# Low parts in four pieces, the second u sooner, a joint first block and sample attention four batches at a time, in a split-fp32 decoder layer

## The reference, cut to what is computed

```
h = h + 0.5 * post1(SwiGLU_1(pre1(h)))
u = pre_m(h);  [qA kA vA qB kB vB gA gB] = u @ w_in
h = h + post_m((sigmoid(gA) * (oA @ p_a) + sigmoid(gB) * (oB @ p_b)) @ w_o)
h = h + 0.5 * post2(SwiGLU_2(pre2(h)))

# oA: dilated sliding-window attention, 3 groups of 4 heads
# oB: stick-breaking attention, 8 heads
# for each of the 8 sample tokens (one per batch): the same two, over
#   211 cached rows of A in three groups, and 2 pages of 128 rows of B
#   found in a page table
```

## Time and profile before

| | |
|---|---|
| median of 3 runs | 1332.63 us (1331.58 to 1333.54) |
| profiled execution | 1329.96 us |
| its span | 1328.1 us |
| mean granted PE clock in it | 0.986 |

### The profile page before, as it was taken

How to read it: one execution, slowest core, us unless ns; L and a number is a source line. 1 busy time by engine, 2 the same in 40 slices (tenths; PEclk the granted TensorE clock), 3 DMA queues, 4 the chain that set the end, 5 groups by cost and what they waited for, 6 DMA issues and landing times.

```text
span 1328.1 us, 24643 instructions
## 1 busy us (share of the span) xinstructions
PE 1271.6 (96%) x10504; PEld 1230.2 (93%) x10504; DVE 555.8 (42%) x925; ACT 411.4 (31%) x683; POOL 453.3 (34%) x131
## 2 busy tenths in 40 slices
PE   6989999999998999999999999998989999999996
PEld 6979999999998999999988888998979999999995
DVE  3373242421226550455377400859484242321225
ACT  6232222122224242345455412244332212222221
POOL 2223334444443233221413312251233444444441
PEclk8989999999998999999999999999999999999998
DMA  5112222222222223312222454221112222222311
GB/s 194 64 64 96 95 95 95 95 79 96 88 76 108 78 85 115 98 33 96 82 79 77 133 189 159 95 96 64 64 64 96 95 95 87 76 84 97 108 57 65
DMA packets 30674, 123.25 MB, mean 93 GB/s; under 512 B 4506, under 2 KB 12722, under 8 KB 18994
## 3 DMA queue, kind: packets, MB, share of 16 engines
q1 hardware_dynamic: 30594, 122.09, 26.5%
HBM read 115.39 MB, written 6.67 MB: 92 GB/s over the span
## 4 chain that ended last, share of the span: by engine, by line
PE 84%; DVE 8%; DVEq 3%; ACT 1%; DMA 1%; issue 1%; POOL 1%; SPq 0%; POOLq 0%; ACTq 0%
PE bank L1398 25%; PE bank L1399 24%; PE bank L1400 24%; DVEq L1043 3%; PE bank L1420 2%; PE bank L1577 1%; DVE u_lo L1059 1%; DVE tmp L1143 1%; PE bank L1766 1%; DVE hid_hi L1131 1%; PE bank L1619 1%; PE bank L1657 1%; PE bank L1606 1%; PE bank L1721 1%; PE bank L1634 1%
## 5 line engine op out<-in xcount | busy, mean ns | idle before, releaser
L580 POOL TENSOR_TENSOR w_lo<-raw,w_hi 128x2048 fp32r<-128x2048 f32 x89 | 409.9, 4607 | 800.3 <-ACT w_hi L647 602.7
L1398 PE MATMUL bank<-u_hi,w_hi 128*128 128x260 f32 x1952 | 562.9, 288 | 19.0 <-DVE u_lo L1059 15.1
L1399 PE MATMUL bank<-u_lo,w_hi 128*128 128x260 f32 x1952 | 553.1, 283 | 0.0
L1400 PE MATMUL bank<-u_hi,w_lo 128*128 128x260 f32 x1952 | 552.4, 283 | 0.0
L1398 PEld LDWEIGHTS bank<-u_hi,w_hi 128*128 128x128 f32 x1952 | 369.1, 189 | 32.5 <-issue 23.4
L1400 PEld LDWEIGHTS bank<-u_hi,w_lo 128*128 128x128 f32 x1952 | 369.7, 189 | 0.0
L1399 PEld LDWEIGHTS bank<-u_lo,w_hi 128*128 128x128 f32 x1952 | 369.4, 189 | 0.0
L647 ACT ACTIVATE w_hi<-raw 128x2048 fp32r<-128x2048 f32 x81 | 154.8, 1911 | 304.6 <-PE bank L1400 303.6
L1398 PE MATMUL bank<-hid_hi,w_hi 128*128 128x260 f32 x704 | 200.6, 285 | 0.5 <-POOL w_lo L594 0.5
L1399 PE MATMUL bank<-hid_lo,w_hi 128*128 128x260 f32 x704 | 200.0, 284 | 0.0
L1400 PE MATMUL bank<-hid_hi,w_lo 128*128 128x260 f32 x704 | 199.8, 284 | 0.0
(11 more groups left out here) (190 smaller groups left out, 1376.6 us busy)
## 6 DMA issues: line engine op xcount, KB each, us to landing
raw<-w_stream SPq DMA_DIRECT2D x84, 1024.0 KB, 4.8
raw<-w_stream SPq DMA_DIRECT2D x8, 768.0 KB, 4.2
e_raw<-w_stream SPq DMA_DIRECT2D x5, 1024.0 KB, 8.4
h<-x_t SPq DMA_DIRECT2D x8, 260.0 KB, 7.6
y_t<-h SPq DMA_DIRECT2D x8, 260.0 KB, 2.3
block<-kb_pool SPq DMA_DIRECT2D x8, 256.0 KB, 3.3
ring<-kb_pool SPq DMA_DIRECT2D x8, 256.0 KB, 3.0
ring<-vb_pool SPq DMA_DIRECT2D x8, 256.0 KB, 4.7
```

The lines of the kernel that those rows point to most:

```text
L580: pool.tensor_tensor(low, w_tiles(slot_of(n) if slot is None else slot)[0], top.bitcast(F32), ALU.subtract).then_inc(lo_made, 1)
L1398: pe.matmul(out, w, hi_x, start=first, stop=False)
L1399: pe.matmul(out, w, lo_x, start=False, stop=False)
L1400: return pe.matmul(out, v, hi_x, start=False, stop=last)
```

## The change

**First block.** x is loaded in four pieces for both groups, ACT and DVE make the high and the low part of u for 520 columns at once, and the first chunk is multiplied for all four banks in one pass over k. Its low parts and those of the second chunk are made by quarters on DVE (`first_lo_part`; ACT makes the high parts by the same quarters in `first_hi_part`). POOL begins with the third chunk.

**Pieces.** Each other low part is made on POOL by instructions of 128 x 512: four for a chunk, two for a half.

**Order on DVE.** In `ffn_up`, `up_scale` is split in the scaling (`up_scale`) and the product with sg (`up_gate`). u_again of group 0 stands after the first tile's hidden instead of the second's, and u_again of group 1 ahead of the last three up_gates. At QKV, u_again of group 1 stands behind all of project_scale(3, ...). `take_out` adds to acc before it writes f, and f's write, not acc's, is what releases the bank, as before.

**Sample attention.** The four batches of a round are the innermost loop in each of the four functions, so consecutive matmuls write at partitions 0, 32, 64 and 96; a call waits for all four batches' pages. Keys of A: one call for four batches at j = 2, 3; keys of B: one call for four batches and one page each at j = 4 to 7; values of A at j = 9, 10; values of B at j = 12 and after the loop. SP waits for a whole round before it loads ring again.

```diff
-            def load_x(g, s):
-                part = (slice(None), slice(2 * s, 2 * s + 2), tg(g))
-                sp.dma_start(h[part], x_t[part]).then_inc(x_in[4 * g + s], 16)
-
             sp.dma_start(gain[:], gains_in).then_inc(gain_in, 16)
             for s in range(4):
-                load_x(0, s)
+                part = (slice(None), slice(2 * s, 2 * s + 2), slice(None))
+                sp.dma_start(h[part], x_t[part]).then_inc(x_in[s], 16)
                 part = (slice(None), slice(s * CH // 4, (s + 1) * CH // 4))
                 sp.dma_start(e_raw[0][part], w_stream[0][part]).then_inc(first_in[s], 16)
             load_early(FFN1 + 1)
-            for s in range(4):
-                load_x(1, s)
             load(2, 0)
             load(3, 1)
...
                 if x >= 4:
-                    sp.wait_ge(ring_used, x - 3)
+                    sp.wait_ge(ring_used, 4)
                 sp.dma_start(ring[x % 4][:, 0:422], ka_cache[x]).then_inc(ring_in[x % 4], 16)
             def load_key_pages(y0, y1):
                 for y in range(y0, y1):
                     if y >= 8:
-                        sp.wait_ge(ring_used, y - 3)
-                        page(kb_pool, y, ring[y % 4], ring_in[y % 4])
+                        half, i = divmod(y - 8, 4)
+                        sp.wait_ge(ring_used, 8 + 4 * half)
+                        page(kb_pool, 8 + 2 * i + half, ring[i], ring_in[i])
                     else:
                         page(kb_pool, y, blocks[4 + y], page_in[y])
...
                     if y < 4:
-                        sp.wait_ge(ring_used, 13 + y)
+                        sp.wait_ge(ring_used, 16)
                     elif y == 4:
-                        sp.wait_ge(va_used, 1)
+                        sp.wait_ge(va_used, 4)
                     elif y >= 12:
-                        sp.wait_ge(ring_used, 17 + y - 12)
+                        sp.wait_ge(ring_used, 20)
                     page(vb_pool, y, blocks[y % 12], page_in[y - 4] if 4 <= y < 12 else ring_in[y % 4])
...
+            def low_part(slot, s, n):
+                src, top, low = w_tiles(slot)
+                a = slice(s * CH // n, (s + 1) * CH // n)
+                return pool.tensor_tensor(low[:, a], src[:, a], top[:, a].bitcast(F32), ALU.subtract)
+
             def lo(n, slot=None):
-                top, low = w_tiles(slot_of(n) if slot is None else slot)[1:]
+                slot = slot_of(n) if slot is None else slot
                 pool.wait_ge(hi_made, n + 1)
-                pool.tensor_tensor(low, w_tiles(slot_of(n) if slot is None else slot)[0], top.bitcast(F32),
-                                   ALU.subtract).then_inc(lo_made, 1)
+                for s in range(4):
+                    made = low_part(slot, s, 4)
+                made.then_inc(lo_made, 1)
...
                 pool.wait_ge(hi_half, count)
-                src, top, low = w_tiles(n % 2)
-                a, b = slice(0, CH // 2), slice(CH // 2, CH)
-                pool.tensor_tensor(low[:, a], src[:, a], top[:, a].bitcast(F32), ALU.subtract)
+                for s in range(2):
+                    low_part(n % 2, s, 4)
                 pool.wait_ge(hi_made, n + 1)
-                pool.tensor_tensor(low[:, b], src[:, b], top[:, b].bitcast(F32), ALU.subtract).then_inc(lo_made, 1)
+                for s in range(2, 4):
+                    made = low_part(n % 2, s, 4)
+                made.then_inc(lo_made, 1)
...
                 dve.wait_ge(post_sq, out_at(p, r, b) + 1)
-                dve.tensor_scalar(f[:, 2 * r + t, tg(g)], out_of(b), gain[:, 2 * p + 1, 2 * r + t:2 * r + t + 1],
-                                  None, ALU.mult).then_inc(read[b], 1)
                 if r == 0 and t == 0:
                     dve.tensor_copy(acc[:, g, :], sqa[:, b, :]).then_inc(acc_added, 1)
                 else:
                     dve.tensor_tensor(acc[:, g, :], acc[:, g, :], sqa[:, b, :], ALU.add).then_inc(acc_added, 1)
+                dve.tensor_scalar(f[:, 2 * r + t, tg(g)], out_of(b), gain[:, 2 * p + 1, 2 * r + t:2 * r + t + 1],
+                                  None, ALU.mult).then_inc(read[b], 1)
                 drain()
...
+            def up_scale(i, b, r):
                 dve.wait_ge(full[b], r + 2 * i + 2)
                 src = psum[b if i else first_bank(1, b)][:, 0:TG]
-                dve.tensor_tensor(x, src, rinv[:, g, :], ALU.mult).then_inc(read[b], 1)
+                dve.tensor_tensor(up_x[b], src, rinv[:, b // 2, :], ALU.mult).then_inc(read[b], 1)
+
+            def up_gate(q, i, b):
                 drain()
                 dve.wait_ge(sg_made, 8 * (q // 2) + 4 * i + b + 1)
-                dve.tensor_tensor(x, x, sg[:, b, :], ALU.mult)
-                hidden(i, b, x)
+                dve.tensor_tensor(up_x[b], up_x[b], sg[:, b, :], ALU.mult)
+                hidden(i, b, up_x[b])
...
-                    up_scale(q, 0, b, r0)
+                    up_scale(0, b, r0)
+                    up_gate(q, 0, b)
                 for b in range(4):
                     gate_scale(1, b, r0)
-                up_scale(q, 1, 0, r0)
-                up_scale(q, 1, 1, r0)
+                up_scale(1, 0, r0)
+                up_gate(q, 1, 0)
                 u_again(q, 0, r0 + FOLD)
-                up_scale(q, 1, 2, r0)
+                for b in range(1, 4):
+                    up_scale(1, b, r0)
                 u_again(q, 1, r0 + FOLD)
-                up_scale(q, 1, 3, r0)
+                for b in range(1, 4):
+                    up_gate(q, 1, b)
...
+            def first_lo_part(n, s):
+
+                dve.wait_ge(*((first_hi, 3 * n + s + 1) if s < 3 else (hi_made, n + 1)))
+                part = slice(s * CH // 4, (s + 1) * CH // 4)
+                src, top, low = w_tiles(slot_of(n))
+                made = dve.tensor_tensor(low[:, part], src[:, part], top[:, part].bitcast(F32), ALU.subtract)
+                made.then_inc(first_lo if s < 3 else lo_made, 1)
+
             for s in range(4):
                 u_low(0, 0, s)
-                part = (slice(None), slice(s * CH // 4, (s + 1) * CH // 4))
-                dve.wait_ge(*((first_hi, s + 1) if s < 3 else (hi_made, 1)))
-                low = dve.tensor_tensor(e_lo[0][part], e_raw[0][part], e_hi[0][part].bitcast(F32), ALU.subtract)
-                low.then_inc(first_lo if s < 3 else lo_made, 1)
+                first_lo_part(FFN1, s)
             for s in range(4):
-                u_low(0, 1, s)
+                first_lo_part(FFN1 + 1, s)
...
+            def first_blocks(q, n, r, blocks):
+
+                g = blocks[0] // 2
+                for b in blocks:
                     pe.wait_ge(read[b], r)
                 if q:
                     pe.wait_ge(lo_made, n + 1)
                 for k in range(KD):
                     pe.wait_ge(u_made, u_at(q, g, k))
-                    if not q and g == 0 and k % 2 == 0:
-                        pe.wait_ge(*((first_lo, k // 2 + 1) if k < KD - 2 else (lo_made, 1)))
+                    if not q:
+                        wait_first_lo(n, k)
                     if q and g == 0 and k == 3:
                         sum_out(q - 1, 1)
-                    for b in (2 * g, 2 * g + 1):
+                    for b in blocks:
                         mm = product(b, slot_of(n), KD, k, tile_cols(b), u_hi, u_lo, k, k == 0, k == KD - 1)
                         if k == KD - 1:
                             mm.then_inc(full[b], 1)
...
+                if not q:
+                    first_blocks(q, n, r, range(4))
                 for g in range(G):
-                    first_blocks(q, n, r, g)
+                    if q:
+                        first_blocks(q, n, r, (2 * g, 2 * g + 1))
                     second_blocks(q, n, r, g)
...
-            def sample_keys_b(y):
-                pe.wait_ge(ring_in[y % 4] if y >= 8 else page_in[y], 16 * (y // 4 + 1) if y >= 8 else 16)
-                slot = ring[y % 4] if y >= 8 else blocks[4 + y]
-                b, pgi = divmod(y, 2)
-                row, col = 32 * (b % 4), (b // 4) * 256 + pgi * P
+                        for i in range(4):
+                            mm = pe.matmul(s1[32 * i:32 * i + AH, rnd * 211 + k0:rnd * 211 + k1],
+                                           qz_a[:, 2 * g + t, 4 * rnd + i, :],
+                                           ring[i][:, t * 211 + k0:t * 211 + k1], start=t == 0, stop=t == 1)
+                            if g == AG - 1 and t:
+                                mm.then_inc(ring_used, 1)
+
+            def sample_keys_b(rnd, pgi):
+
+                for i in range(4):
+                    if rnd:
+                        pe.wait_ge(ring_in[i], 16 * (3 + pgi))
+                    else:
+                        pe.wait_ge(page_in[2 * i + pgi], 16)
                 for t in range(4):
-                    mm = pe.matmul(s2[row:row + BH, col:col + P], qz_b[:, t, b, :], slot[:, t * P:(t + 1) * P],
-                                   start=t == 0, stop=t == 3)
```

(35 more changed lines are left out.)

113 lines of the change are left out of this document (62 added, 51 removed).

## The result

The changed kernel takes 1300.03 us (median of 4 runs, 1297.17 to 1300.25) against 1332.35 before (4 runs): a ratio of 0.9749, 95% interval 0.9733 to 0.9765, so 32.3 us faster. The forecast was 1293 with a range of 1286 to 1309; direction and range held, the gain was 39 in the forecast and is 32 in the runs. The profiled execution took 1299.87 us.

A forecast was written before the change was run, and what follows sets the result against it. PE, busy 96% of the span, was taken as the bound, with 33.6 us of waits, half-clock stretches and a serial sample loop left to gain. Terms summed to 39.6 us, giving 1293 us, range 1286 to 1309.

The forecast's parts named there:

- the signs named: Trace signs of a right forecast: e_lo wait gone, no half clock from 15 to 25, sample loop about 65 us.
- I take 1.29: POOL's low parts: a 128x512 instruction takes 1.29 us, by the slope between 2048 and 1024 columns.
- free of a 4.6 us block: 1.1: QKV's u_again: u_again(1,1) comes one scaling later but escapes a 4.6 us block; gain 1.1 us.
- u_agains of FFN1 and FFN2: Start of both FFN phases: u_again comes earlier, a new stall of some 1.6 us follows; net gain 2.0 us each.
- Ends of phases: Gains of 5.8 us at FFN1's end, 2.8 at the mixer's end, 2.1 for sqb and small waits, 0.2 at FFN2's end.
- f comes later now and acc sooner: Mixer's end: of 5.0 us of waits for f and acc, a gain of 2.8 us was taken.
- First block: Kernel start: PE's 5.49 us e_lo wait and 2.17 lost to half clock go, first matmul 0.3 later; gain 7.4 us.
- Sample attention: Sample loop: concurrent matmuls save 26.8 us of work, new waits and one clock drop cost 10.6; gain 16.2 us.
- The first rival: Sample loop: column tiles take turns, so it gains nothing and new waits of 2 us stay: 1311 us, chance 0.07.
- wait for the whole row of pieces: Rival on the pieces: POOL's next piece starts before DVE gets the port, 15.8 us lost: 1309 us, chance 0.08.
- transfers cost what was said: Against a rival that SP's single queue also delays weight chunks, with more clock drops: 8 us more, 1301, chance 0.15.
- the fourth rival: Steady loop: pieces above 2.35 us make w_lo late in some 88 chunks; at 2.6 about 1382 us, chance 0.02.

The follow-up runs named there:

- pieces_only: The kernel before with one edit, POOL's low parts in instructions of 512 columns: 1322.44 us, ratio 0.9920 to the kernel before.
- whole_pool: The changed kernel with POOL's low parts whole again (2048 columns, halves of 1024): 1314.24 us, ratio 0.9854 to the kernel before.
- pool_waits: The changed kernel, POOL beginning each phase's sixth chunk's low part only after u_again of group 1: 1299.53 us, ratio 0.9749 to the kernel before.
- old_u_order: The changed kernel with ffn_up's order of before, pieces kept: 1300.72 us, ratio 0.9753 to the kernel before.
- f_first: The changed kernel with f ahead of acc as before, pieces kept: 1300.95 us, ratio 0.9759 to the kernel before.

## Why the prediction was right, and where it was short

**What bounds the kernel**, waits of PE and a serial sample loop: right; every place named moved. Of the signs named, PE's wait for e_lo, the clock from 15 to 25 us and the 4 us wait for ring<-kb_pool came out as said; the sample loop is 68.5 us long and not 65.

**The pieces.** "I take 1.29" measured 1.33 as a mean, 1.27 where DVE is quiet. That a DVE operation comes in between two POOL instructions was right at FFN1's end (5.6 for 5.8; pieces_only, whole_pool). PE's wait for acc there was to be 0.2 and 1.3 us and is 1.4 in two parts. The Trainium skill, "SBUF — State Buffer", section "SBUF: two separate sides", says that the lock is held for the whole instruction and the other blocks. The lengths above (3.50 for 1.3, 6.09 for 5.05) agree. It doesn't say who comes next: here the two take turns.

**The step that failed** is "free of a 4.6 us block: 1.1" for QKV. I priced the release of one blocked operation by the length of the block. The prediction itself had the right rule, "a row of DVE operations beside POOL runs at one operation for 1.3 us", and did not apply it to the row of f and u_lo there. DVE at that place, first before, where one POOL instruction starts at 480.07, then in the changed kernel, where the first of four pieces starts at 467.36:

```profile
480.85 5.02 DVE L1059 SCALAR_TENSOR_TENSOR u_lo<-f,gain,u_hi 128x260 fp32r<-128x260 f32 x2
485.79 0.68 DVE L1068 TENSOR_TENSOR f<-h,rinv 128x520 f32<-128x520 f32 x1
```

```profile
467.08 2.41 DVE L1082 TENSOR_TENSOR f<-h,rinv 128x520 f32<-128x520 f32 x2
469.57 2.75 DVE L1073 SCALAR_TENSOR_TENSOR u_lo<-f,gain,u_hi 128x260 fp32r<-128x260 f32 x2
472.25 1.77 DVE L1082 TENSOR_TENSOR f<-h,rinv 128x520 f32<-128x520 f32 x1
```

Before, one u_lo took 4.62 us and the rest ran alone; now four operations wait about 1 us each. The last f of the row ends 6.4 us after POOL's start before and 6.7 after it now, so the end is no sooner: PE waits 3.1 us in three parts, where it was 2.4. With POOL whole and the new order one f takes 5.07 us, and PE waits 2.8 us at once. And behind each of these PE runs at half clock for longer: 475.0 to 479.9 in the changed kernel, 478.7 to 484.2 in whole_pool, 485.0 to 489.9 in pieces_only, each with 23 to 25 matmul records, where before there were 12:

```profile
486.10:489.10 3.00, 2.82 (x12) 2.30 (x12) 2.76 (x6) 1.92 (x6) 0.00 (x0) 0.50 0.00 0
```

That is 1.4 us of the 2.1; why the clock came back sooner before, no run tells. pool_waits shows what makes the waits: without POOL beside it the site gains 3.6 us over the changed kernel and 1.5 over the one before, where the forecast was 1.1. At the u_agains of FFN1 and FFN2 (1.8 and 1.4 for 2.0) the new stall behind the up_gates was foreseen and came, 0.8 and 0.5 us of waits for sg; cutting alone gave 0.6 at each, the rest is the order's by old_u_order's trace.

**Ends of phases.** Right in sum (5.6 for 5.8, 3.2 for 2.8). For "f comes later now and acc sooner" I had no more than a choice; whole_pool shows that the pieces decide it, and f_first that with them the order counts for little.

**First block.** Short by 0.7: the first matmul comes at 8.77 instead of 7.54, 1.2 us later and not 0.3. ACT's first u_hi begins 0.8 us later (5.03 for 4.21), since the first transfer is twice as large, where my working counted only the widths of ACT's and DVE's operations.

**Sample attention.** 12.3 for 16.2. The work saved was 26.8 in the forecast; measured it is 20.6 of busy time plus 3.9 hidden by the two stretches at half clock (half of 3.00 and of 4.70), 24.4. New waits were 8.6 in the forecast and are 8.3; the largest was to be 4.5 and is 4.1, keys of A 2.0 and 3.1. The clock was put at 2 and cost 3.9. So the mechanism was right and two terms were mis-sized: the work saved by 2.4 us, and the clock by 1.9, with two drops and not one. The 2.4 can be laid out call by call, from the first start of a call to the next start of the fill item. The sample matmuls took 35.7 us before and not 37.7: keys and values of B held PE for 12.6 and 12.8 us, not for the 13.6 each that the row's 0.106 gave, since where two batches met their matmuls overlapped already. And they take 11.8 us now at full clock and not 10.9, 0.99 for a call of 32 and not 0.9. Fewer changes between calls and fill items give some 0.5 back. The first rival (column tiles take turns) is out: starts are 7 ns apart with all 128 partitions of contraction in use, so the rule on row groups in the Trainium skill, "TensorE: Matmul & The Clock Gate", section "The mechanism", is not what decides for column tiles. That page's figure of 3.07 for four row tiles, in its section "Why this matters for your kernels", comes close here: 3.15 us to 0.99 is 3.2 times, 35.7 to 11.8 is 3.0 times.

**The rivals.** DVE did not wait for the whole row of pieces, transfers cost what was said, and PE waited only 1.0 us for w_lo in the whole run: the steady loop's spare time covers the pieces.

**Slips in the prediction's sums**, none of which moves the forecast by more than 0.1 us: the spare time of a chunk is 11.5 - 1.9 - 4.6 = 5.0 us and not 4.8, the last keys' wait, 4 + 3.5 - 2.9, is 4.6 and not 4.5, and FFN1's end adds up to 5.9 and not 5.8. In the fourth rival a piece would have to be above (11.5 - 1.9) / 4 = 2.4 us, which is at its far bound and not below it, and pieces of 2.6 would cost 0.8 and not 1.0 us for each chunk, some 1363 in all.

## What to carry to other kernels

Cutting a long GpSimd instruction helps a lone VectorE operation that waits behind it. With a row of them it helped little or nothing here: the two engines take turns, and the row ends near the sum of both. So place the GpSimd work where nothing late stands behind VectorE, and follow what it lands on. When a batched form of a loop waits for all its inputs at once, count the issue time of each transfer and the slots that come free together before the gain in work; here they took a third of it. A change of order that is worth little beside another edit (0.9 us within noise for acc ahead of f) can lose without it (3.3 us at the mixer's end): try both alone.

## What the runs showed of the hardware

POOL's subtract costs 4607 ns on 2048 columns, 2421 on 1024, 1329 on 512 and 778 on 256, waits included. Beside it a cast of one tensor waits too (1.23 us for 0.30, and 4.65 in the earlier trace rows), so it isn't only operations on two tensors. Four plain fp32 matmuls at output partitions 0, 32, 64 and 96, each with 128 rows of contraction, start 7 ns apart, and a call of 32 records takes 0.99 us where 32 took 3.15. At QKV's u_again PE ran at half clock for 3.0 us behind waits of 2.4 us, and for 4.9 to 5.5 behind waits of 2.8 to 3.1. But in the sample loop it was 3.0 behind a wait of 3.1 and 4.7 behind one of 4.1, so the length of the wait alone doesn't tell how long the clock stays down. A transfer whose page comes from the page table costs SyncE about 1.1 us to issue.
